# Two tiles of the gated merge move into the long convolution, and its table copies go

## The chip, the cores and the metric

One core of a Trainium2 chip runs the whole program in one launch. The metric is the device time of one execution in microseconds. The engines are TensorE (PE: matmuls and transposes), VectorE (DVE), ScalarE (ACT), GpSimd (POOL) and SyncE (SP), which only issues DMAs here. Each runs its own list of instructions in order, and they meet through semaphores.

## The reference

The program is a first block (layer norms, gated attention, a chunked recurrence, a feed-forward part) and a second one, for 512 tokens of width 1024 in float32. What matters here is the second block's mixer:

```python
y_na = neighbourhood_attention(...)            # 512 x 512
for n in range(2):                             # y_hy, 512 x 512
    z = gates[n] * long_conv_bidir(z, filt[:, 0, n], filt[:, 1, n], bias[n])
m = sigmoid(g_na) * (y_na @ w_na_o) + sigmoid(g_hy) * (y_hy @ w_hy_o)
x = x + g1 * (m @ w_out)
```

`y_na` is known before the convolution starts. `y_hy` is the result of its second pass (n = 1). The long convolution is done as products with tables of cosines and sines: forward into 512 frequencies, a product with the filter's spectrum, and back.

## The kernel before

**Arithmetic.** Every float32 product is split: each operand x becomes a high part (ScalarE rounds it to `fp32r`, a copy) and a low part (VectorE subtracts the high part from x), and TensorE forms high·high, high·low and low·high. `mm3` (L570 to L573) issues these three matmuls, one line each. `tile` (L600) is one 128 x 512 output tile: it waits for the weight's low part, takes one of TensorE's eight PSUM banks in rotation (waiting until its last content has been read), and issues 3 matmuls for each block of 128 of the contraction.

**Weights.** 1 MB pieces number 0 to 119 (`J_...`) go through three buffers `raw`. SyncE's `weights(upto)` issues the loads in order, each after the piece three before it has its low part. ScalarE's `high(upto)` and VectorE's `low_parts(upto)` split them in the same order, `low_parts` in 128 x 2048 subtractions. Most pieces alternate between two pairs `whi`/`wlo`; some (`OWN`) have a place of their own, given by `ahead`. A shared place is free when TensorE has passed `used` of the piece two before it.

**The long convolution** (`for n in range(2)`). The pieces J_DFT2 and J_DFT2 + 1 (77 and 78) hold the forward and the backward table. In pass n TensorE issues 16 forward products in four groups of frequencies f (`forward`), then 4 backward tiles `hi` (`back`): f = 0 for all four, f = 1 for all four, then f = 2 and 3 tile by tile. Between them, for each f, VectorE multiplies four times with the spectrum (signal `hp`), GpSimd forms two sums (`hsum`), ScalarE takes the high parts and VectorE the low parts `yy`. After pass 0 VectorE multiplies the `hi` tiles with a gate and filters (`hz`, source `x1` beside the banks), GpSimd sums, and ScalarE and VectorE split the sums into `zh` and `zl` (named `xrr` in the profile), the four inputs of pass 1; TensorE's first group of pass 1 goes through these inputs one after the other as they become ready. After pass 1 the tiles are combined (`kk`), gated and split to `zh`, `zl` again.

For pass 0 the tables lie in the shared places. After its part of pass 0 ScalarE copies all four halves (two high, two low) into `tabs` (signal `tab`), and pass 1 reads them there, so that the shared places are free for the merge's first weights. The copies stand on ScalarE between the high parts of pass 0's last frequencies and those of `zh`.

**The merge.** Its weights are J_MERGE (79, first half of the columns of w_na_o), 80 (first half of w_hy_o), 81 and 82 (second halves). For each half, `src` 0 takes `nh`, `nl` (the split y_na, named `Xr`) and `src` 1 takes `zh`, `zl`; each gives 4 tiles of 12 matmuls, and k numbers 8 output tiles. For each k the gates come from DRAM (`gd`, loaded by GpSimd's queue into `tq`), ScalarE takes the sigmoid, VectorE multiplies it with the bank (L2559), GpSimd adds the two sources, and ScalarE and VectorE split the sum into `tabs` again. ScalarE's `high` of piece 82 stands behind the high part of merged tile 3. Then the product with w_out begins (`J_OUT`), with `tabs` as moving operand.

**Loads.** SyncE issues 16 loads `kk` for the eight (n, f) with the three merge weights behind those of the seventh. GpSimd loads the row `bcg` behind the sums of the convolution.

Of the kernel before, what the change touches and what calls it, by code (L numbers as in the profile page):

```python
# [207 lines left out]
J_FAST = J_UP2 + 2  # L208
OWN = (*J_AHEAD, *range(J_TAP, J_TAP + 4), *range(J_FAST, J_FAST + N_FAST))
SHARED = [j for j in range(J_DOWN2 + 11) if j not in OWN]  # L210

# [82 lines left out]
def build(nc, ins, out):  # L294
    with ExitStack() as ctx:
# [15 lines left out]
        def flat(x):  # L311
            return x[:, :, :].rearrange("p a b -> p (a b)")
# [100 lines left out]
        with ExitStack() as c0:  # L413
# [77 lines left out]
        ahead = {J_WO + 3: (flat(qa_r), flat(ka_r)), J_UP + 2: (flat(qa_r), flat(ka_r)), J_K2: (flat(qn_r), flat(qt_r)),  # L491
                 J_UP2: (flat(cl), flat(act2_r[:, 0:4, :]))}

# [65 lines left out]
        def tensor_program(eng):  # L559
# [488 lines left out]


            for n in range(2):  # L1050
                if n == 0:
                    weights(J_DFT2)
                else:
                    pe.wait_ge(sig["tab"], 4)
                (fh, fl), (gh, gl_) = [parts_of(J_DFT2 + c) for c in range(2)] if n == 0 else tabs

# [46 lines left out]
                if n == 0:  # L1103
                    weights(J_DFT2 + 1)
                for k in range(4):
                    take(("hi", n, k), "hz", 24 + 3 * k + 2 if n else 16 + 4 * (k // 2) + 3 + k % 2)
# [6 lines left out]
                if n == 0:  # L1113
                    used(J_DFT2)
                    used(J_DFT2 + 1)


            for cgp in range(2):
                for src, (yh, yl, part) in enumerate(((nh, nl, "nh"), (zh, zl, "z1"))):
                    j = J_MERGE + 2 * cgp + src  # L1120
                    pe.wait_ge(sig["sp_lo"], split_no(part, 3))
                    for m in range(4):
                        tile(j, ("mg", src, 4 * cgp + m), "mg_m", 8 * cgp + 4 * src + m + 1, yh, yl, 0, m, nk=4, width=512)
                    used(j)
# [83 lines left out]
        def scalar_program(eng):  # L1208
# [22 lines left out]
            def high(upto):  # L1231

                while conv[0] <= min(upto, len(conv_at) - 1):
# [3 lines left out]
                    if j in (J_WO + 3, J_UP + 2):  # L1237
                        ac.wait_ge(sig["pe"], at["w", J_WO + 3 if j > J_WO + 3 else J_WO])
                    elif j == J_TAP:
                        ac.wait_ge(sig["h_ke"], 2)  # L1240
                        ac.wait_ge(sig["h_qe"], 2)
                    elif j == J_K2:
                        ac.wait_ge(sig["sp_lo"], split_no("down0", 7))
                    elif j == J_UP2:
                        ac.wait_ge(sig["pe"], at["w", J_MERGE + 3])
                    elif j in (J_DOWN2, J_DOWN2 + 1):
                        ac.wait_ge(sig["pe"], at["fast", N_FAST - 1 if j > J_DOWN2 else N_FAST - 2, last_of(N_FAST - 1 if j > J_DOWN2 else N_FAST - 2)])
                    elif j >= 2 and j != J_TAP + 1:
                        ac.wait_ge(sig["pe"], at["w", used_by(j)])
                    if j == J_DFT2 + 2:  # L1250
                        ac.wait_ge(sig["tab"], 4)
                    act(parts_of(j)[0], raw[i % 3][:, :], ACT.Copy, "whi")
# [414 lines left out]
            def mirrored_part(k):  # L1667
# [4 lines left out]
                act(bt[k % 2], b[:, 256:512], ACT.Copy, "zu")  # L1672

            def last_high(k):
                ac.wait_ge(sig["hz"], 24 + 3 * k + 3)
                act(zh[:, k, :], tq[k][:, :], ACT.Copy, "sp_hi")

            for n in range(2):
                if n:
                    tile(("hi", 0, 3))  # L1680
                for f in range(4):
                    sums_high(n, f)
                if n == 0:
                    for b in range(2):
                        ac.wait_ge(sig[f"tb{b}"], 16 * TB_ALL)
                    for c in range(2):
                        for i, x in enumerate(parts_of(J_DFT2 + c)):
                            act(tabs[c][i][:, :], x.bitcast(F32), ACT.Copy, "tab")
                for k in range(4):
# [6 lines left out]
                    else:  # L1696
                        mirrored_part(k)
                        if k:
                            last_high(k - 1)
                if n == 0:  # L1700
                    high(J_MERGE + 1)
                else:
                    last_high(3)
# [119 lines left out]
        def vector_program(eng):  # L1823
# [656 lines left out]
            for n in range(2):  # L2480
# [20 lines left out]
                sums_low(n, 3)  # L2501
                if n:
                    low_parts(J_MERGE)

# [46 lines left out]
            for cgp in range(2):  # L2551
                for src in range(2):
                    low_parts(J_MERGE + 2 * cgp + src + 1)
                    for m in range(4):
                        k = 4 * cgp + m
                        b = tile(("mg", src, k))
                        q = 4 + k % 3 if src else m
# [157 lines left out]
        def gpsimd_program(eng):  # L2715
# [222 lines left out]
            po.wait_ge(sig["gated"], 32)  # L2938
            po.wait_ge(sig["pe"], at["yt", 3])
            po.e.dma_start(bcg[:, :], rows_of(gated, 0)).then_inc(sig["rows"], 16)  # L2940
            def gate_first(k):
# [12 lines left out]
            for k in range(8):  # L2954
                po.wait_ge(sig["mg_m"], 8 * (k // 4) + 4 + k % 4 + 1)
                add(tq[k % 4][:, :], tq[4 + k % 3][:, :], tq[k % 4][:, :], ALU.add, "mg_a")
                if k < 5:
                    gate_second(k + 3)
                if k in (1, 2, 3):
                    gate_first(k + 3)  # L2960
# [51 lines left out]
        def sync_program(eng):  # L3012
# [72 lines left out]
            for k in range(8):  # L3085
                if k >= 3:
                    sp.wait_ge(sig["hp"], 4 * (k - 2))
                for i in range(2):
                    sp.e.dma_start(kk_[k % 3][:, i, :], kd[k // 4, 4 * i + k % 4]).then_inc(sig[f"kk{k % 3}"], 16)
                if k == 6:  # L3090
                    weights(conv_at[J_MERGE + 1] + 1)
            for k in range(4):
# [160 lines left out]
```

## Time and profile before

| | us |
|---|---|
| Median of 3 runs (1613.34 to 1614.63) | 1613.46 |
| The profiled execution | 1612.63 |
| its span in the trace | 1610.8 |
| TensorE busy | 1557.2 |
| granted clock of TensorE, mean | 0.993 |

The span runs from the first to the last instruction of the trace; all times of the rows are microseconds from its start. The profiled execution took 1.8 us more than its span. A matmul's length in the timeline includes its way through the array, so that consecutive ones overlap: what one costs in a row of many is the distance between their starts. The stretch that the diff touches lies between 1086 and 1199 us: attention ends at about 1092, pass 0 of the convolution lasts until 1120, pass 1 until 1155, and the merge until 1199.

### The profile page before, as it was taken

The numbers are of one execution on the slowest core, as the hardware profiler recorded it, in microseconds if no ns is written. First come the engines' busy times: TensorE is split into PE (matmuls) and PEld (weight loads), VectorE is DVE, ScalarE is ACT, GpSimd is POOL, SyncE is SP. The second block draws the span as 40 slices with busy tenths as digits, with TensorE's granted clock in tenths as the row PEclk, the third lists the DMA queues.
The fourth block names the chain that finished last, engine by engine and source line by source line (L and its number), as shares of the span: only waits on it lengthen the run. The fifth ranks groups of instructions, "written<-read, shape, count | busy, mean of one in ns | idle before, by whom it ended". The sixth has DMA issues, their size and how long they took to land. (4 is left out here: it accounts for less than half of the span.)

```text
span 1610.8 us, 21154 instructions
## 1 busy us (share of the span) xinstructions
PE 1557.2 (97%) x8536; PEld 1316.3 (82%) x8536; DVE 1006.4 (62%) x1453; ACT 698.7 (43%) x1022; POOL 429.0 (27%) x371
## 2 busy tenths in 40 slices
PE   6999998999999999999999999998899999999997
PEld 5768886788888887888988778886788999999886
DVE  7676456878887576325675643437864688885334
ACT  5644346736433333323623344444445544443322
POOL 0024325523421010000150022214332655550002
PEclk9999999999999999999999999999999999999999
DMA  7342112451444254321446432305452122224221
GB/s 301 105 144 92 66 72 79 158 212 75 157 167 149 108 205 157 105 105 66 142 158 260 133 99 90 115 34 177 147 192 106 53 106 105 106 105 157 82 76 53
DMA packets 46684, 202.05 MB, mean 125 GB/s; under 512 B 14480, under 2 KB 14736, under 8 KB 27962
## 3 DMA queue, kind: packets, MB, share of 16 engines
q1 hardware_dynamic: 37346, 172.04, 29.6%
q0 software_dynamic: 8704, 28.30, 5.0%
q8 instruction: 68, 1.11, 0.3%
q10 hardware_dynamic: 536, 0.35, 0.1%
q14 instruction: 30, 0.25, 0.0%
HBM read 179.67 MB, written 21.00 MB: 125 GB/s over the span
## 5 line engine op out<-in xcount | busy, mean ns | idle before, releaser
L571 PE MATMUL ps<-xh,whi 128*128 128x512 f32 (+1 forms) x1136 | 403.0, 355 | 11.3 <-DVE xl L1887 8.5
L572 PE MATMUL ps<-xl,whi 128*128 128x512 f32 (+1 forms) x1136 | 398.2, 350 | 0.0
L573 PE MATMUL ps<-xh,wlo 128*128 128x512 f32 (+1 forms) x1136 | 397.6, 350 | 0.0
L1843 DVE TENSOR_TENSOR wlo<-raw,whi 128x2048 fp32r<-128x2048 f32 x91 | 222.3, 2443 | 143.9 <-ACT whi L1213 143.8
L1213 ACT ACTIVATE whi<-raw 128x512 fp32r<-128x512 f32 (+1 forms) x193 | 236.8, 1231 | 160.1 <-PE ps L573 90.0
L571 PEld LDWEIGHTS ps<-xh,whi 128*128 128x128 f32 x1136 | 216.1, 190 | 51.9 <-issue 22.2
L573 PEld LDWEIGHTS ps<-xh,wlo 128*128 128x128 f32 x1136 | 215.1, 189 | 30.0
L572 PEld LDWEIGHTS ps<-xl,whi 128*128 128x128 f32 x1136 | 215.3, 190 | 27.6
L2719 POOL TENSOR_TENSOR act<-xr 128x512 f32<-128x512 f32 x22 | 39.9, 1817 | 198.2 <-DVE xr L2285 197.6
L2285 DVE SCALAR_TENSOR_TENSOR xr<-ps,pc,xr 128x511 f32<-128x511 f32 x88 | 65.2, 747 | 40.8 <-ACT xr L1213 39.3
L2615 DVE TENSOR_TENSOR wlo<-raw,whi 128x512 fp32r<-128x512 f32 x98 | 79.0, 838 | 0.0
L1213 ACT ACTIVATE xr<-ps,pc 128x512 f32<-128x512 f32 x44 | 34.0, 772 | 94.1 <-PE ps L573 94.0
L573 PE MATMUL ps<-whi,al 128*128 128x512 f32 x176 | 69.8, 397 | 0.0
L571 PE MATMUL ps<-whi,ah 128*128 128x512 f32 x176 | 69.8, 397 | 0.0
L572 PE MATMUL ps<-wlo,ah 128*128 128x512 f32 x176 | 69.8, 397 | 0.0
L1213 ACT ACTIVATE xr<-xr 128x512 f32<-128x512 f32 (+1 forms) x31 | 23.5, 757 | 83.7 <-DVE xr L2285 59.0
L2152 DVE TENSOR_SCALAR cl<-ps,st 128x64 f32<-128x64 f32 x32 | 9.0, 281 | 73.8 <-PE ps L816 73.8
L571 PE MATMUL ps<-whi,xh 128*128 128x512 f32 x128 | 52.0, 407 | 1.1 <-DVE vr L1958 1.1
L2719 POOL TENSOR_TENSOR tq<-tq 128x512 f32<-128x512 f32 x28 | 39.8, 1439 | 49.1 <-DVE tq L2559 22.0
L2634 DVE TENSOR_TENSOR xr<-ps,xr 128x256 f32<-128x256 f32 (+1 forms) x63 | 33.8, 536 | 30.4 <-PE ps L573 29.9
L572 PE MATMUL ps<-wlo,xh 128*128 128x512 f32 x128 | 50.7, 396 | 0.0
L573 PE MATMUL ps<-whi,xl 128*128 128x512 f32 x128 | 50.7, 396 | 0.0
(468 smaller groups left out, 3500.7 us busy)
## 6 DMA issues: line engine op xcount, KB each, us to landing
raw<-in_w_in SPq DMA_DIRECT2D x35, 1024.0 KB, 5.2
raw<-in_ffn_w SPq DMA_DIRECT2D x33, 1024.0 KB, 4.8
raw<-in_ada SPq DMA_DIRECT2D x24, 1024.0 KB, 4.8
raw<-in_w_up SPq DMA_DIRECT2D x22, 1024.0 KB, 5.0
raw<-in_w_down SPq DMA_DIRECT2D x11, 1024.0 KB, 4.7
xd<-X POOLq DMA_DIRECT2D x8, 512.0 KB, 6.6
td<-vr POOLq DMA_DIRECT2D x16, 256.0 KB, 3.5
raw<-td SPq DMA_DIRECT2D x4, 1024.0 KB, 4.8
```

The lines of the kernel that those rows point to most:

```text
L571: pe.e.matmul(o, lh, rh, start=start, stop=False)
L572: pe.e.matmul(o, lh, rl, start=False, stop=False)
L573: return pe.e.matmul(o, ll, rh, start=False, stop=stop)
L1213: m = ac.e.activation(dst, src, func, **more)
L1843: up(ve.e.tensor_tensor(lo, raw[conv_at[j] % 3][:, :], hi.bitcast(F32), ALU.subtract), "wlo")
L2152: up(ve.e.tensor_scalar(dst, b[:, hcol:hcol + 64], st[:, i % 32, 3:4], None, ALU.mult), "at_o")
L2285: up(ve.e.scalar_tensor_tensor(out=y[:, o], in0=b[:, i], scalar=pcol(name + "_w", n * w + c), in1=y[:, o], op0=ALU.mult, op1=ALU.add), "cv ...
L2615: up(ve.e.tensor_tensor(lo, product_source(n, p), hi.bitcast(F32), ALU.subtract), "wlo")
L2634: up(ve.e.tensor_tensor(dst, b, s, ALU.add), "f_a")
L2719: po.e.tensor_tensor(dst, a, b, op).then_inc(sig[signal], 1)
```

## The change

Two of the merge's sixteen tiles (source 0, tiles 0 and 1) are computed inside the convolution: tile 0 on TensorE behind pass 0, tile 1 in pass 1 between the forward and the backward part. ScalarE copies their banks into `x1`, from where VectorE's later product with the sigmoid reads them. The pieces 79 and 80 get places of their own: 79 where the table copies were, 80 in `bc` and `cl`. The four copies of the tables go, and both passes read the shared places. On ScalarE the high part of piece 79 stands where the copies were; VectorE takes its low part at the end of pass 0's frequencies, and the low part of 80 at the end of pass 1's. Loads of 79, 80 and 81 are issued behind the third, fifth and seventh pair of `kk`. The load of `bcg` moves to GpSimd's fifth step of the merge.

The places of the pieces:

```diff
-OWN = (*J_AHEAD, *range(J_TAP, J_TAP + 4), *range(J_FAST, J_FAST + N_FAST))
+OWN = (*J_AHEAD, J_MERGE, J_MERGE + 1, *range(J_TAP, J_TAP + 4), *range(J_FAST, J_FAST + N_FAST))
...
-                 J_UP2: (flat(cl), flat(act2_r[:, 0:4, :]))}
+                 J_UP2: (flat(cl), flat(act2_r[:, 0:4, :])),
+                 J_MERGE: (tabs[1][0][:, :], tabs[1][1][:, :]), J_MERGE + 1: (bc_r[:, :], flat(cl))}
```

TensorE's program:

```diff
+            def first_merge(m):
+                tile(J_MERGE, ("mg", 0, m), "tab", m + 1, nh, nl, 0, m, nk=4, width=512)
...
-                else:
-                    pe.wait_ge(sig["tab"], 4)
-                (fh, fl), (gh, gl_) = [parts_of(J_DFT2 + c) for c in range(2)] if n == 0 else tabs
+                (fh, fl), (gh, gl_) = [parts_of(J_DFT2 + c) for c in range(2)]
...
                 if n == 0:
                     weights(J_DFT2 + 1)
+                else:
+                    first_merge(1)
                 for k in range(4):
                     take(("hi", n, k), "hz", 24 + 3 * k + 2 if n else 16 + 4 * (k // 2) + 3 + k % 2)
...
                 if n == 0:
-                    used(J_DFT2)
-                    used(J_DFT2 + 1)
+                    first_merge(0)
+            used(J_DFT2)
+            used(J_DFT2 + 1)
...
-                    for m in range(4):
+                    for m in range(0 if src or cgp else 2, 4):
```

ScalarE's:

```diff
+                    elif j == J_MERGE:
+                        for b in range(4):
+                            ac.wait_ge(sig[f"tb{b}"], 16 * TB_ALL)
+                        ac.wait_ge(sig["pe"], at["yt", 3])
...
+            def first_merged(m):
+                b = tile(("mg", 0, m))
+                ac.wait_ge(sig["hz"], 24)
+                act(x1[:, m, :], b[:, :], ACT.Copy, "tab")
...
                     sums_high(n, f)
+                    if n and f == 1:
+                        first_merged(1)
                 if n == 0:
-                    for b in range(2):
-                        ac.wait_ge(sig[f"tb{b}"], 16 * TB_ALL)
-                    for c in range(2):
-                        for i, x in enumerate(parts_of(J_DFT2 + c)):
-                            act(tabs[c][i][:, :], x.bitcast(F32), ACT.Copy, "tab")
+                    high(J_MERGE)
...
                 if n == 0:
+                    first_merged(0)
                     high(J_MERGE + 1)
```

VectorE's:

```diff
-                if n:
-                    low_parts(J_MERGE)
+                low_parts(J_MERGE + n)
...
-                        b = tile(("mg", src, k))
+                        if src or k >= 2:
+                            b = tile(("mg", src, k))
+                        else:
+                            ve.wait_ge(sig["tab"], m + 1)
+                            b = x1[:, m, :]
```

GpSimd's:

```diff
-            po.wait_ge(sig["pe"], at["yt", 3])
-            po.e.dma_start(bcg[:, :], rows_of(gated, 0)).then_inc(sig["rows"], 16)
...
+                if k == 4:
+                    po.wait_ge(sig["pe"], at["w", J_MERGE + 1])
+                    po.e.dma_start(bcg[:, :], rows_of(gated, 0)).then_inc(sig["rows"], 16)
```

SyncE's:

```diff
-                if k == 6:
-                    weights(conv_at[J_MERGE + 1] + 1)
+                if k in (2, 4, 6):
+                    weights(conv_at[J_MERGE + k // 2 - 1])
```

## Rows read from the trace of the kernel before

**Rows 1.** The page: span; busy time of TensorE, its share, instructions.
```profile
span 1610.8 us, 21154 instructions
...
PE 1557.2 (97%) x8536; PEld 1316.3 (82%) x8536; DVE 1006.4 (62%) x1453; ACT 698.7 (43%) x1022; POOL 429.0 (27%) x371
```

**Rows 2.** Windows: length, busy time (instructions) per engine, PEclk, DMA share, GB/s.
```profile
1090.00:1155.00 65.00, 52.87 (x273) 43.03 (x272) 56.17 (x77) 29.88 (x38) 29.84 (x22) 0.97 0.44 147
1155.00:1250.00 95.00, 95.00 (x436) 78.02 (x435) 55.09 (x67) 47.47 (x65) 28.77 (x31) 1.00 0.44 155
1148.50:1152.00 3.50, 3.50 (x19) 3.50 (x18) 3.14 (x4) 0.38 (x1) 0.00 (x0) 0.52 0.99 310
```

**Rows 3.** Timeline, TensorE: start, length, instruction; in brackets idle and releaser.
```profile
1120.20 0.40 PE L573 MATMUL ps<-yy,wlo 128*128 128x512 f32 x1
...
1122.89 0.47 PE L571 MATMUL ps<-xrr,tab 128*128 128x512 f32 x1 [2.29 <-DVE xrr L1857]
...
1128.82 0.50 PE L571 MATMUL ps<-xrr,tab 128*128 128x512 f32 x1 [0.88 <-DVE xrr L1857]
...
1135.52 0.39 PE L573 MATMUL ps<-xrr,tab 128*128 128x512 f32 x1
...
1137.43 0.36 PE L571 MATMUL ps<-tab,yy 128*128 128x256 f32 x1 [1.52 <-DVE yy L1857]
...
1142.13 0.39 PE L571 MATMUL ps<-tab,yy 128*128 128x256 f32 x1 [1.61 <-DVE yy L1857]
...
1154.75 0.39 PE L571 MATMUL ps<-Xr,whi 128*128 128x512 f32 x1
...
1165.67 0.40 PE L571 MATMUL ps<-xrr,whi 128*128 128x512 f32 x1
...
1187.81 0.40 PE L571 MATMUL ps<-xrr,whi 128*128 128x512 f32 x1
...
1199.01 0.39 PE L571 MATMUL ps<-whi,tab 128*128 128x512 f32 x1
```

**Rows 4.** Timeline, VectorE, convolution and merge.
```profile
1117.89 2.48 DVE L2519 TENSOR_TENSOR tq<-ps,ch 128x512 f32<-128x512 f32 x4 [2.51 <-PE ps L573]
1120.71 1.29 DVE L2519 TENSOR_TENSOR tq<-ps,ch 128x512 f32<-128x512 f32 x2 [0.33 <-PE ps L573]
1122.05 2.38 DVE L1857 TENSOR_TENSOR xrr<-tq,xrr 128x512 fp32r<-128x512 f32 x2
...
1137.21 2.47 DVE L2498 TENSOR_TENSOR tq<-ps,kk 128x512 f32<-128x512 f32 x4
...
1158.17 1.48 DVE L1857 TENSOR_TENSOR xrr<-tq,xrr 128x512 fp32r<-128x512 f32 x2
...
1182.47 2.29 DVE L1843 TENSOR_TENSOR wlo<-raw,whi 128x2048 fp32r<-128x2048 f32 x1 [1.11 <-ACT whi L1213]
```

**Rows 5.** Timeline, ScalarE, convolution and merge.
```profile
1114.20 1.90 ACT L1213 ACTIVATE tab<-whi 128x2048 fp32r<-128x2048 f32 x1
...
1127.94 3.70 ACT L1213 ACTIVATE whi<-raw 128x2048 fp32r<-128x2048 f32 x2
...
1139.89 0.63 ACT L1213 ACTIVATE yy<-tq 128x512 fp32r<-128x512 f32 x1 [2.49 <-POOL tq L2719]
...
1163.56 1.30 ACT L1213 ACTIVATE tq<-tq 128x512 f32<-128x512 f32 x2 [2.17 <-DMA tq<-gd]
1165.93 1.92 ACT L1213 ACTIVATE whi<-raw 128x2048 fp32r<-128x2048 f32 x1 [1.07 <-PE ps L573]
```

**Rows 6.** Timeline, GpSimd, end of the first convolution.
```profile
1119.26 2.53 POOL L2719 TENSOR_TENSOR tq<-tq 128x512 f32<-128x512 f32 x2 [5.63 <-DVE tq L2519]
1122.08 1.80 POOL L2719 TENSOR_TENSOR tq<-tq 128x512 f32<-128x512 f32 x1 [0.28 <-DVE tq L2519]
```

**Rows 7.** Timeline, SyncE's DMA queue.
```profile
1086.73 25.88 SPq L3089 DMA_DIRECT2D kk<-kd  x14
```

**Rows 8.** By tile, the weights w_na_o: issue to landing.
```profile
DMA to landing us min/median/max: 8.5/10.5/12.4
```

More of the change, by code:

```diff
@@ L1247, in high @@
                         ac.wait_ge(sig["pe"], at["fast", N_FAST - 1 if j > J_DOWN2 else N_FAST - 2, last_of(N_FAST - 1 if j > J_DOWN2 else N_FAST - 2)])
-                    elif j >= 2 and j != J_TAP + 1:
+                    elif j == J_MERGE:
+                        for b in range(4):
+                            ac.wait_ge(sig[f"tb{b}"], 16 * TB_ALL)
+                        ac.wait_ge(sig["pe"], at["yt", 3])
+                    elif j >= 2 and j not in (J_TAP + 1, J_MERGE + 1):
                         ac.wait_ge(sig["pe"], at["w", used_by(j)])
-                    if j == J_DFT2 + 2:
-                        ac.wait_ge(sig["tab"], 4)
                     act(parts_of(j)[0], raw[i % 3][:, :], ACT.Copy, "whi")
```

## The prediction

> **What bounds the kernel now.** I read the page first: TensorE is busy in 97% of the span [rows 1], so only a change that takes work or a wait off TensorE's own list can move the end. Then the windows: from 1090 to 1155 us it is busy in 52.87 of 65, and from 1155 to 1250 in 95 of 95 [rows 2]. So the convolution is bound by the chain of TensorE, VectorE, GpSimd and ScalarE, while in the merge TensorE works without a pause. The timeline of TensorE shows the pauses that the diff aims at. Its last backward matmul of pass 0 starts at 1120.20, and pass 1 begins at 1122.89 after 2.29 us idle; its first group has another pause of 0.88 ahead of 1128.82. The last forward matmul of pass 1 starts at 1135.52, the backward part at 1137.43 after 1.52, and its second frequency at 1142.13 after 1.61 [rows 3]. All are waits for low parts from VectorE. Last I read the other engines around these places [rows 4 to 6].
>
> **The tiles leave the merge.** Four tiles of source 0 take 1154.75 to 1165.67, 10.92 us, so one takes 2.73, and the two that go give 5.46 [rows 3]. That is the whole gain if the places where they are put cost nothing.
>
> **Tile 0, behind pass 0.** TensorE is free for it about 0.23 (estimate, one matmul's distance: 2.73 / 12) behind 1120.20, at 1120.43, and done at 1123.2. Pass 1 began at 1122.89, so its first matmuls are 0.3 late. The pause of 0.88 before the fourth input's products at 1128.82 takes this up [rows 3]: cost 0. Without that cover it would be 0.3. Its weights must be split by then. ScalarE's high part stands where the first table copy started, 1114.20, and takes 1.90 [rows 5]; the low part takes 2.29 [rows 4] and so ends at about 1118.5, 1.9 before TensorE needs it. The load is issued behind three pairs of `kk` that start at 1086.73 [rows 7]; even with the longest landing of this tensor, 12.4 [rows 8], it has landed long before 1114.
>
> **Tile 1, in pass 1.** It starts at 1135.75 and ends at 1138.5, 1.05 behind the old start of the backward part at 1137.43. The rotation of banks also moves on by two: the fourth `hi` bank is now one whose content is read by the third product of the block that VectorE starts at 1137.21 and ends at 2.47 later [rows 4], so about 1139.1, and `take` stands ahead of all four tiles. The backward part then starts near 1139.2, 1.8 late, where the pause before 1142.13 covers 1.61 [rows 3]. That leaves 0.2, which the like pause of the third frequency (VectorE's same loop) takes up, so cost 0; bounds 0 and 0.2, and the whole 1.8 if those pauses were not there. ScalarE's copy of the bank stands before the high part that starts at 1139.89 after 2.49 idle [rows 5]; TensorE ends the tile at 1138.5, the copy needs 0.6, and it fits with half a microsecond to spare. In pass 0 the other copy replaces ScalarE work: only one of the two 128 x 2048 copies of 3.70 at 1127.94 stays [rows 5].
>
> **The cost: VectorE at the end of pass 0.** The four table copies were ScalarE's, and the first high part behind them was not what VectorE waited for: VectorE came to it from its own products at 1122.05 [rows 4]. Taking the copies away therefore gives nothing on the chain. The new 2.29 low part does cost. It runs from about 1116.2 to 1118.5, and the block of four products that started at 1117.89 (after 2.51 idle) starts 0.6 late; that ends at 1121.0 where the next block started at 1120.71, so the chain is 0.25 to 0.3 late [rows 4]. Behind it stand the low parts of pass 1's inputs. There two subtractions took 2.38 where two others took 1.48 [rows 4], and GpSimd's sum beside them took 1.80 where two took 2.53, 1.27 each [rows 6]; they met. A shifted meeting can cost another 0.9 or save that. So the delay d of all of pass 1 lies between -0.6 and 1.15; I take 0.6, near the middle of the unlucky half, since the sums are now closer to the subtractions.
>
> The row shows that the two collide. The Trainium skill (SBUF — State Buffer, "Who interferes with whom") says why: a VectorE operation with both inputs in SBUF and a GpSimd operation that reads SBUF exclude each other, each for its whole length. By that rule the long low part would block GpSimd for 2.29 if a sum fell into it, and the two products that now read `x1` in place of a bank become such operations too; by the rows GpSimd is idle for 5.63 before 1119.26 [rows 6], so the sum by the rule stays as it is, with d at 0.6.
>
> **The merge.** TensorE enters it at 1154.75 + 0.6, does two tiles, then source 1 from 1160.8, for which the last low part of pass 1 is there at 1158.17 + 1.48 + 0.6 = 1160.3 [rows 3, 4]. Then tiles 4 to 7 until it needs piece 82 at 1187.81 - 5.46 + 0.6 = 1182.95 [rows 3]. Its low part started at 1182.47 and took 2.29, ending 1184.8, 3.0 before use [rows 4]; unmoved, it would now cost 1.8. But it moves: ScalarE's high part of piece 81 waited for TensorE at 1165.93, although its sigmoids at 1163.56 were done by 1164.86 [rows 5]. The new condition is met at 1155, and the sigmoids' own wait for a load is shorter by some tenths because the 1 MB loads come earlier. So the chain from there on is 1.1 to 1.8 ahead, and piece 82 is ready between 1183.0 and 1183.7. I take a wait of 0.1; bounds 0 and 1.8. What follows (product with w_out, norms, feed-forward) waits for TensorE and moves as one. `bcg` is loaded later, but used only behind the product with w_out. Queue entries on GpSimd: one less in the convolution, one more in the merge, where it waits for VectorE anyway.
>
> Sum at an unchanged clock: 5.46 - 0.6 - 0.1 = 4.8.
>
> **The clock.** From 1148.5 to 1152.0 the granted clock was 0.52, the lower of its two levels (1.2 GHz) [rows 2]. It fell after a stretch with three pauses of 1.5 us and more. Its 19 matmuls of 256 columns took 3.50. At full clock they would take 2.3 (estimate: 24 of them run from 1137.43 to 1142.13 - 1.61 = 1140.5, 0.12 each) [rows 2, 3], so 1.2 was lost. With tile 1 the two pauses ahead of this shrink from 3.1 to about 0.7, so I expect the drop to go. The gain is not whole: piece 82's chain hangs on ScalarE's and VectorE's work, and TensorE runs into it earlier, so I give back half. 4.8 + 0.6 = 5.4.
>
> The Trainium skill (TensorE: Matmul & The Clock Gate, "What's actually happening") has the clock follow how busy TensorE has recently been. By it the drop goes, as here; without it the sum stays at 4.8.
>
> **From the profile to the median.** The sum is made against the profiled execution of 1612.63, whose span is 1610.8. The median of the runs is 1613.46, 0.8 more, and the difference is taken from that: 1613.46 - 5.4 = 1608.1.
>
> **Rivals.**
> A (the forecast): tiles hidden, the clock drop gone. 1608.1, chance 0.40; its own range 1607 to 1609.3.
> B: tiles hidden, the drop stays, since other pauses of pass 1 stay. 4.8 less, 1608.7, chance 0.30.
> C: the merge turns from TensorE's to the gates' chain (loads of `gd`, sigmoid, product, sum, split, then piece 82). For it: the sigmoids at 1163.56 waited for a load [rows 5], and that wait is set by the z parts of pass 1, which move later, not earlier. Against it: 1.1 us of room in front of 1165.93. If piece 82 is ready no sooner than before, TensorE starts on it at 1184.8 in place of 1187.81: 3.0 gained, 1610.4. Chance 0.17.
> D, slower: piece 79's split is late. TensorE and VectorE take their lists in order, and both have work of pass 1 behind it; on VectorE these are the four products of 1117.89, so it costs from there. A landing at L gives a low part that ends at L + 1.90 + 2.29 + 0.1, and pass 1 is late by what this is beyond 1118.2 (1117.89 and the 0.33 idle before 1120.71) [rows 4, 5]. The 5.46 are eaten up when L is 1119.4. A load issued where the fourteenth `kk` ends, 1086.73 + 25.88 = 1112.61, would be there at 1123.1 with 10.5 us landing [rows 7, 8]: 9.2 late, 3.7 slower than before, 1617.2. Against it: the issue stands behind the third pair, not the seventh. Chance 0.05.
> E: more than A, when the meeting of VectorE and GpSimd falls well and the whole 1.2 of the clock is kept: 6.6, 1606.9. Chance 0.08.
>
> **The numbers.** The range goes from 1606.6 to 1611.0: E's end below and C's above. A difference under 0.2%, 3.2 us, can't be told from none. Faster by more: A, B, E and nearly none of C, 0.77. Within: C and the upper end of B, 0.18. Slower: 0.05.
>
> **What would show it.** The pauses before 1122.89 and 1137.43 hold twelve matmuls each. The first products of VectorE behind pass 0 start some 0.6 later; the first matmul of the fourth input of pass 1 at 1129.1 to 1129.9. The merge begins at about 1155 and w_out's product at 1193.5 to 1194.5. PEclk is 1.00 in pass 1's backward part (A) or not (B). A pause ahead of piece 82 over 1 us is C. A pause ahead of tile 0 is D. I am wrong if w_out's product starts at the forecast time but the end does not follow, or if pass 1 grows by more than 2 us.

## The result, and the profile after

The changed kernel takes 1608.47 us (median of 7 runs, 1606.93 to 1611.45), the kernel before 1614.3 beside it (7 runs, 1612.93 to 1616.39). The ratio is 0.9972, interval 0.9961 to 0.9983: faster, by 2.7 to 6.3 us. A second comparison, later, gave 1610.48 (11 runs) against 1614.17 (33 runs), 0.9974 [0.9965, 0.9983]. The forecast was 1608.1, 5.4 less than the 1613.46 that the kernel before had then.

The profiled execution took 1610.57, and its page shows TensorE as busy as before [rows 1]:

```profile
span 1608.8 us, 21150 instructions
...
PE 1558.5 (97%) x8536; PEld 1316.6 (82%) x8536; DVE 1002.3 (62%) x1453; ACT 692.4 (43%) x1020; POOL 428.8 (27%) x371
```

The windows of the profile after (columns as in [rows 2]): the convolution's window has 57.67 us of TensorE where it had 52.87, and the clock is low behind 1148.5 here too. The last two lie outside the change.

```profile
1090.00:1155.00 65.00, 57.67 (x294) 47.05 (x294) 57.06 (x76) 24.07 (x35) 29.32 (x21) 0.97 0.43 146
1155.00:1250.00 95.00, 95.00 (x457) 78.79 (x456) 53.95 (x72) 50.70 (x72) 29.28 (x32) 1.00 0.48 171
1148.50:1152.00 3.50, 3.02 (x18) 2.82 (x19) 3.50 (x4) 0.69 (x2) 0.00 (x0) 0.80 0.73 212
515.00:535.00 20.00, 20.00 (x93) 18.02 (x93) 7.04 (x9) 2.57 (x2) 2.54 (x2) 0.66 0.43 159
1275.00:1285.00 10.00, 8.79 (x61) 8.82 (x62) 9.28 (x11) 4.90 (x10) 6.21 (x4) 0.83 0.31 107
```

TensorE's timeline after, which answers to [rows 3] (first and last matmul of each tile moved, and the matmul behind it):

```profile
1122.18 0.39 PE L572 MATMUL ps<-Xr,tab 128*128 128x512 f32 x1
...
1124.76 0.39 PE L574 MATMUL ps<-Xr,tab 128*128 128x512 f32 x1
1124.99 0.40 PE L572 MATMUL ps<-xrr,whi 128*128 128x512 f32 x1
...
1130.62 0.49 PE L572 MATMUL ps<-xrr,whi 128*128 128x512 f32 x1 [0.85 <-DVE xrr L1868]
...
1137.72 0.39 PE L572 MATMUL ps<-Xr,tab 128*128 128x512 f32 x1
...
1140.30 0.39 PE L574 MATMUL ps<-Xr,tab 128*128 128x512 f32 x1
1141.15 0.35 PE L572 MATMUL ps<-whi,yy 128*128 128x256 f32 x1 [0.47 <-DVE tq L2509]
...
1148.75 0.38 PE L572 MATMUL ps<-whi,yy 128*128 128x256 f32 x1 [1.66 <-DVE yy L1868]
...
1156.56 0.40 PE L572 MATMUL ps<-Xr,tab 128*128 128x512 f32 x1
...
1162.17 0.39 PE L572 MATMUL ps<-xrr,bcr 128*128 128x512 f32 x1
...
1184.27 0.39 PE L572 MATMUL ps<-xrr,whi 128*128 128x512 f32 x1
...
1195.46 0.39 PE L572 MATMUL ps<-whi,tab 128*128 128x512 f32 x1
```

No pause stands ahead of 1124.99, where 2.29 us stood; ahead of the backward part 0.47 is left of 1.52, and the 1.61 behind it is gone. From 1156.56 on there is no pause. VectorE after, which answers to [rows 4]:

```profile
1098.91 4.87 DVE L2509 TENSOR_TENSOR tq<-ps,kk 128x512 f32<-128x512 f32 x8 [0.57 <-issue]
...
1117.87 2.29 DVE L1854 TENSOR_TENSOR tab<-raw,tab 128x2048 fp32r<-128x2048 f32 x1 [0.75 <-ACT tab L1218]
1120.08 3.67 DVE L2529 TENSOR_TENSOR tq<-ps,ch 128x512 f32<-128x512 f32 x6
1123.67 0.86 DVE L1868 TENSOR_TENSOR xrr<-tq,xrr 128x512 fp32r<-128x512 f32 x1
1124.69 1.55 DVE L1868 TENSOR_TENSOR xrr<-tq,xrr 128x512 fp32r<-128x512 f32 x1 [0.15 <-ACT xrr L1218]
...
1159.77 1.48 DVE L1868 TENSOR_TENSOR xrr<-tq,xrr 128x512 fp32r<-128x512 f32 x2
...
1181.72 2.29 DVE L1854 TENSOR_TENSOR wlo<-raw,whi 128x2048 fp32r<-128x2048 f32 x1 [1.11 <-ACT whi L1218]
```

And GpSimd's three sums beside the two subtractions [rows 6]:

```profile
1121.44 4.24 POOL L2733 TENSOR_TENSOR tq<-tq 128x512 f32<-128x512 f32 x3 [6.07 <-DVE tq L2529]
```

**A yardstick finer than the runs.** Runs of one kernel differ by 3 to 11 us, single terms are under 3. So I measure a *stretch* in each trace: from the first of the last sixteen transposes of the attention (`ps<-ident,cl`; 1092.02 before, 1093.41 after) to w_out's first matmul (1199.01 and 1195.46). It is 106.99 before and 102.05 after: 4.94 shorter. The span is only 2.0 shorter, since the start lies 1.39 later and the way from w_out to the end takes 413.34 in place of 411.79. Both have a clock row. From 515 to 535 us the clock is 0.66, where the kernel before has 0.74:

```profile
515.00:535.00 20.00, 20.00 (x100) 17.90 (x99) 7.45 (x10) 3.35 (x3) 2.53 (x2) 0.74 0.41 159
```

TensorE's matmul number 2401 starts at 484.27 (484.46 before), number 2801 at 574.20 (572.80 before), so 1.59 is lost between them. From 1275 to 1285 the clock is 0.83, and 1.00 before. Offsets below ("+37.21") count from the stretch's start.

### The profile page after: what moved, and what is told of

Its sections match the earlier page's. It is cut to its first block and busy times, and to the rows that moved or that the text cites. A ratio compares the mean times of both kernels' runs of the same rounds, so it can differ in the third digit from the quotient of the medians.

```text
span 1608.8 us, 21150 instructions
## 1 busy us (share of the span) xinstructions
PE 1558.5 (97%) x8536; PEld 1316.6 (82%) x8536; DVE 1002.3 (62%) x1453; ACT 692.4 (43%) x1020; POOL 428.8 (27%) x371
## 5 line engine op out<-in xcount | busy, mean ns | idle before, releaser
L1854 DVE TENSOR_TENSOR wlo<-raw,whi 128x2048 fp32r<-128x2048 f32 x89 | 217.5, 2444 | 142.5 <-ACT whi L1218 142.4
L1218 ACT ACTIVATE whi<-raw 128x512 fp32r<-128x512 f32 (+1 forms) x191 | 233.0, 1223 | 156.8 <-PE ps L574 86.8
```

What stands on the lines that cost most here:

```text
L1218: m = ac.e.activation(dst, src, func, **more)
L1854: up(ve.e.tensor_tensor(lo, raw[conv_at[j] % 3][:, :], hi.bitcast(F32), ALU.subtract), "wlo")
```

## The experiments

Each is the changed kernel with the edit shown (ScalarE's copies of the banks and VectorE's reading of them follow it); "pause 5" is TensorE's 1.6 us ahead of the third frequency of pass 1's backward part (1148.75 above).

**Tile 0 alone.**
```diff
-                else:
-                    first_merge(1)
...
-                    for m in range(0 if src or cgp else 2, 4):
+                    for m in range(0 if src or cgp else 1, 4):
```


> Only tile 0 stands in the convolution (behind pass 0); tile 1 is back in the merge; places, loads and splits are those of the change. The stretch from the last transposes of attention to the first matmul with w_out was 106.99 us before and 102.05 with the change. Theory (each tile is hidden wholly, 2.73 us each): 104.8 us, and a time 2.7 us above the change's. Rival (the gain comes from the places and loads, not the tiles): 102 to 102.5. Rival (tile 0 is the one that costs, since pass 1 is a chain): 106.5, no gain left over from it.

Measured: stretch 104.46, 2.53 shorter than before, with the clock low (0.51 from 1148.5 to 1152), near the theory's 104.8; from w_out on 413.34. The runs: 1613.57, ratio 0.9997 [0.9987, 1.0006].

**Tile 1 alone.**
```diff
-                if n == 0:
-                    first_merge(0)
...
-                    for m in range(0 if src or cgp else 2, 4):
+                    for m in (range(4) if src or cgp else (0, 2, 3)):
```


> Only tile 1 stands in the convolution (pass 1), tile 0 is in the merge. Theory: the same 104.8 us for the stretch as with tile 0 alone; the pause ahead of pass 1 is back (about 2.3 us) and the wait for the bank ahead of the backward part stays at 0.4 to 0.5. Rival (tile 1 costs through the rotation of banks): 105.5 to 106.

Measured: stretch 103.19, below theory and rival, since the clock is full at 1150; the pause ahead of pass 1 is back with 2.30, the one ahead of the backward part is 0.47. The clock is low here behind the 2.30, in pass 1's first group, where consecutive matmuls start 0.43 apart and not 0.23. The fourth input comes at +37.08 even so, 0.28 later than before, of which 0.25 come from pass 0: the pause ahead of it took the low clock's loss up. Runs: 1611.87, 0.9996 [0.9985, 1.0007].

**No tile moved, the table copies gone, piece 79 split in pass 0.**
```diff
-                    first_merge(0)
...
-                    first_merge(1)
...
-                    for m in range(0 if src or cgp else 2, 4):
+                    for m in range(4):
```


> Neither tile stands in the convolution; the table copies are gone and pieces 79 and 80 have their places, loads and splits as in the change. This shows what the rest of the change costs or gives by itself. Theory: the stretch takes 107.4 us, 0.4 to 0.5 more than before: 0.36 for the store of the gates that VectorE's first products wait for (the early 1 MB load shares the DMA engines with it), about 0.05 for the low part in pass 0. Rival (the copies' removal gives something): under 106.7. Rival of the prediction (VectorE's low part costs 0.6 or more): over 107.9.

Measured: stretch 107.48, 0.49 longer than before; pauses 2.30, 0.86, 1.34, 1.61, 1.66 in pass 1. Runs: 1614.78, 1.0002 [0.9989, 1.0014]. Pass 0 came 0.19 late here (below), so what the change does beside the tiles costs another 0.3, of which 0.03 shows at the fourth input; the rest lies in source 0's first four tiles (11.25 against 10.92), and why is open. It gains nothing. Against this kernel, each with its lateness of pass 0 taken off, tile 0 gives 2.83 and the two give 5.58, all three at the low clock at 1150: about their own 2.73 each. Both are hidden whole, and they add up. The runs' medians couldn't have told this: they place both single tiles level with before. Part of that is the low clock at 1275 to 1285, which both have and which takes some 1.5 back behind the stretch; the rest is open.

**Pause 5 filled** with seven matmuls whose result the next tile overwrites.
```diff
+                if n:
+                    h, _ = weights(J_MERGE)
+                    pe.wait_ge(sig["tab"], 2)
+                    for q in range(7):
+                        pe.e.matmul(bank["mg", 0, 1][:, :], h[:, P * q:P * q + P], nh[:, 0, :], start=True, stop=True)
                 for k in range(4):
                     for f in (2, 3):
                         back(f, k)
```


> The change with seven matmuls of 512 columns more whose results are overwritten, ahead of the third frequency's backward part of pass 1, where TensorE waits 1.66 us. Theory of the prediction (the clock drop at about 1150 follows from TensorE's pauses in pass 1): the drop to 0.5 is gone from 1148 to 1156, the backward part ends 1.2 us earlier, and the stretch is 101.0 to 101.6. Rival (the drop does not hang on these pauses): the drop is there and the stretch 102.0 to 102.2, no pause to fill being left over 0.1.

Measured: the drop is gone, as the theory has it, the stretch is 100.89 (1.16 less than the change's, of which 0.34 is that pass 0 isn't late here), and there is a pause that the change doesn't have, for the low part of piece 82:

```profile
1184.86 0.51 PE L572 MATMUL ps<-xrr,whi 128*128 128x512 f32 x1 [0.34 <-DVE wlo L1859]
```

Runs: 1610.33, 0.9983 [0.9973, 0.9992].

**The low part of piece 79 computed twice**, the second time as the change does.
```diff
+                if n == 0:
+                    ve.wait_ge(sig["whi"], conv_no(J_MERGE))
+                    ve.e.tensor_tensor(tabs[0][1][:, :], raw[conv_at[J_MERGE] % 3][:, :], parts_of(J_MERGE)[0].bitcast(F32), ALU.subtract)
                 low_parts(J_MERGE + n)
```


> The change with one more 128 x 2048 subtraction (2.29 us) on VectorE just ahead of piece 79's low part in pass 0, its result unused. The change's own low part moved VectorE's next products by 0.44 us but pass 1's fourth input by only 0.05. Theory (the first 0.3 to 0.4 vanish in the meeting of VectorE's and GpSimd's SBUF operations, everything beyond goes through): the products start 2.2 later and the stretch from attention's last transposes to the first matmul with w_out grows from 102.05 to 104.0 to 104.3, with a new pause ahead of tile 0. Rival (there is more room in the chain): under 103.

Measured, on VectorE and at the two pauses of TensorE in pass 1:

```profile
1118.99 2.29 DVE L2515 TENSOR_TENSOR tab<-raw,tab 128x2048 fp32r<-128x2048 f32 x1 [0.75 <-ACT tab L1218]
1121.20 2.28 DVE L1854 TENSOR_TENSOR tab<-raw,tab 128x2048 fp32r<-128x2048 f32 x1
1123.40 3.07 DVE L2532 TENSOR_TENSOR tq<-ps,ch 128x512 f32<-128x512 f32 x5
```
```profile
1127.98 0.47 PE L572 MATMUL ps<-xrr,whi 128*128 128x512 f32 x1 [1.37 <-DVE xrr L1868]
...
1133.91 0.50 PE L572 MATMUL ps<-xrr,whi 128*128 128x512 f32 x1 [0.86 <-DVE xrr L1868]
```

The fourth input comes at +39.04 where tile 0 alone has +36.88: 2.16 of the extra 2.2 go through. VectorE has no slack behind pass 0. The new pause is ahead of pass 1 (1.37), not ahead of tile 0 as expected. The stretch is 103.51, between theory and rival, with full clock at 1150 and at 1275; runs 1611.05, 0.9983 [0.9972, 0.9995].

**The load of piece 79 issued behind all pairs of `kk` but the last.**
```diff
-                if k in (2, 4, 6):
-                    weights(conv_at[J_MERGE + k // 2 - 1])
+                if k == 6:
+                    weights(conv_at[J_MERGE + 1] + 1)
```


> The change with the loads of pieces 79, 80 and 81 all behind the seventh pair of kk loads, where they stood before. Rival D of the prediction, made to happen: the load of 79 lands some 8 to 12 us after about 1114, ScalarE's and VectorE's split and with them the products behind pass 0 start 8 to 9 us late; the stretch is 109.5 to 111.5 against 106.99 before and 102.05 with the change, and the kernel is 1 to 4 us slower than before. Rival (the load is faster here because nothing is beside it, landing in 5 us): 105 to 106.5, still a gain.

Measured: the load was issued at 1111.68; ScalarE waited for it, and TensorE stood ahead of tile 0, not of pass 1:

```profile
1118.38 1.92 ACT L1218 ACTIVATE tab<-raw 128x2048 fp32r<-128x2048 f32 x1 [5.07 <-DMA raw<-in_w_nao]
```
```profile
1122.68 0.79 PE L572 MATMUL ps<-Xr,tab 128*128 128x512 f32 x1 [3.05 <-DVE tab L1854]
```

It landed 6.7 us after its issue. The fourth input came at +42.02, 4.8 later than in the change and 5.2 later than before. The stretch is 106.87, between theory and rival, and the runs 1613.32, 0.9997 [0.9988, 1.0006]: the gain is gone, and not more. Rival D's mechanism is real; it had 9.2 late, of which 3.8 are the landing of 10.5 in place of 6.7.

**A third tile in pause 5.**
```diff
+                if n:
+                    tile(J_MERGE, ("mg", 0, 2), "mg_m", 3, nh, nl, 0, 2, nk=4, width=512)
                 for k in range(4):
                     for f in (2, 3):
                         back(f, k)
...
-                    for m in range(0 if src or cgp else 2, 4):
+                    for m in range(0 if src or cgp else 3, 4):
```


> The change with a third tile (tile 2 of source 0) on TensorE ahead of the third frequency's backward part of pass 1, where it waits 1.66 us; its bank is read later as before. Theory (what is left is bound by the chain behind pass 1, whose last low part ends 0.9 ahead of its use, and by piece 82, ready 0.25 ahead): TensorE comes to source 1 early and waits 1 to 2 us there; the stretch is 101.6 to 102.2, the third tile giving nearly nothing. Rival (each tile put into a pause gives 2.73 less its overshoot of 0.8): 100.1 to 100.3.

Measured: full clock at 1150, and two pauses in the merge, the first somewhat above the theory's 1 to 2 us:

```profile
1156.67 0.50 PE L572 MATMUL ps<-xrr,bcr 128*128 128x512 f32 x1 [2.20 <-DVE xrr L1870]
...
1179.71 0.51 PE L572 MATMUL ps<-xrr,whi 128*128 128x512 f32 x1 [0.66 <-DVE wlo L1856]
```

Stretch 101.24, 0.35 longer than with pause 5 filled for nothing; runs 1610.69, 0.9979 [0.997, 0.9988]. Of the tile's 2.73, 2.20 is waited for ahead of source 1, whose last low part doesn't come sooner (+66.90 here, +66.84 with pause 5 filled).

**Third tile in two halves, in pause 5 and behind the backward part; the loads of 79 and 80 both behind the fourth pair of `kk`, piece 82 split one tile earlier.**
```diff
+            def third_merge(k0):
...
+                for k in range(k0, k0 + 2):
+                    a = 512 * k + 2 * P
+                    o = mm3(b[:, :], h[:, a:a + P], l[:, a:a + P], nh[:, k, :], nl[:, k, :], k == 0, k == 3)
...
+                if n:
+                    third_merge(0)
                 for k in range(4):
                     for f in (2, 3):
                         back(f, k)
+                if n:
+                    third_merge(2)
...
-                    for m in range(0 if src or cgp else 2, 4):
+                    for m in range(0 if src or cgp else 3, 4):
...
-                if k in (2, 4, 6):
-                    weights(conv_at[J_MERGE + k // 2 - 1])
+                if k in (3, 4, 6):
+                    weights(conv_at[J_MERGE + k // 2 - (k > 3)])
...
+                    if m == 2 and cgp == 0:
+                        high(J_MERGE + 3)
...
+                        if k == 3 and src:
+                            low_parts(J_MERGE + 3)
```


> The change with three edits: the load of piece 79 one pair of kk later (theory: gives back the 0.36 us that VectorE waits for the store of the gates), piece 82 split before merged tile 0 (ScalarE) and before merged tile 3's low part (VectorE), and the first six of tile 2's twelve matmuls in the 1.66 us pause of pass 1, the other six behind pass 1. Theory: the stretch is 100.7 to 101.0 if the clock drop at about 1150 is there, 100.0 to 100.3 if not, against 102.05 and 100.89. Rival (nothing left to gain, source 1's input sets the pace): 101.7 or 100.5.

Measured: the stretch is the shortest, 100.28, as foreseen for a full clock at 1150, with no pause ahead of piece 82. But from w_out on it takes 420.62. TensorE, ScalarE and the windows there:

```profile
1211.37 0.79 PE L572 MATMUL ps<-whi,tab 128*128 128x512 f32 x1 [4.99 <-DVE wlo L1871]
```
```profile
1188.90 0.63 ACT L1233 ACTIVATE tq<-tq 128x512 f32<-128x512 f32 x1 [4.35 <-DMA tq<-gd]
...
1202.31 0.63 ACT L1233 ACTIVATE tq<-tq 128x512 f32<-128x512 f32 x1 [5.99 <-DMA tq<-gd]
```
```profile
1200.00:1205.00 5.00, 5.00 (x23) 4.03 (x22) 1.51 (x3) 1.67 (x3) 0.14 (x1) 1.00 1.00 374
1210.00:1216.00 6.00, 4.63 (x11) 3.67 (x12) 3.52 (x2) 0.79 (x1) 0.00 (x0) 0.50 0.58 216
```

The early split does two things. It frees a buffer, so w_out's 1 MB load goes out at 1182.22 (1184.04 in the change). And it holds VectorE, so GpSimd waits 1.64 us for VectorE and issues its 256 KB load of gates at 1183.09 (1180.90 in the change, ahead of the big load). Issued behind the big load, the gates take 5.8 us to land, where they took 3.5 in the change:

```profile
1183.09 0.55 POOL L2975 DMA_DIRECT2D tq<-gd  x1 [1.64 <-DVE tab L1885]
```

The next gates load is therefore issued at 1195.95, beside 2 MB of `X<-xd`, and takes 6.3. Behind it hangs the next split of w_out, 4.99 us late, and behind the pause the clock is 0.50. Runs: 1612.93, 0.9994 [0.9982, 1.0007].

**The change again.** The same kernel, unedited.

> The changed kernel itself, beside other runs of the one before, for the size of the gain and a second profile. Theory: 0.9970 to 0.9975 of the time before (4 to 5 us less); the stretch from attention's last transposes to the first matmul with w_out is 101.7 to 102.1 where the clock drop at about 1150 is there and 100.9 to 101.0 where it is not. Rival (the gain of the first seven runs was luck of the clock): under 2.5 us less.

Measured: neither of the two. Stretch 102.34 at full clock from 1148 to 1156, with a wait for piece 82:

```profile
1148.00:1156.00 8.00, 7.24 (x54) 6.81 (x55) 7.79 (x13) 3.18 (x7) 0.03 (x1) 1.00 0.86 286
1275.00:1285.00 10.00, 9.26 (x65) 9.29 (x65) 9.26 (x10) 4.79 (x9) 6.51 (x4) 0.83 0.31 107
```
```profile
1183.70 0.50 PE L572 MATMUL ps<-xrr,whi 128*128 128x512 f32 x1 [0.94 <-DVE wlo L1854]
```
```profile
1098.68 4.88 DVE L2509 TENSOR_TENSOR tq<-ps,kk 128x512 f32<-128x512 f32 x8 [1.09 <-issue]
```

Of this kernel there are thus two traces, one with the low clock and one without. From the backward part to source 1 the first takes 21.02 (1141.15 to 1162.17), the second 19.37 (1141.03 to 1160.40): with the low clock it takes 1.65 more (0.08 of it pause 5). From source 1 to w_out the first takes 33.29, the second 34.60: 1.31 comes back, 0.94 of it as this pause, the rest without a pause of its own. The last row shows why the stretch is no shorter even so: VectorE's first products started 0.52 later still than in the first trace.

**Before again.** The kernel before, unedited.

> The kernel before, for a second profile. Theory: the stretch is again 106.9 to 107.1 with the clock drop at about 1150 or 105.7 without; from the first matmul with w_out to the end it took 411.8 in its first profile and 413.3 in that of the change and of five of its variants, always with a clock drop at 1275 to 1285. Theory: that drop has nothing to do with the change, and falls on this kernel too in some executions (413.3). Rival: the kernel before always shows 411.8, and the change brings the drop.

Measured: stretch 107.02 with the low clock at 1150, 411.81 from w_out on, both within 0.03 of the first trace. So the low clock at 1275 to 1285 is again absent, as the rival has it; two traces don't settle whether this kernel ever has it. Runs: 1612.52 (8 runs), 0.9996 [0.9985, 1.0007] against the others of the same kernel: the method finds no difference where there is none.

**The third tile in halves and the moved loads, piece 82 as in the change.** The edit of the two halves without its last two hunks.

> The last version without the early split of piece 82: the load of 79 one pair later and six of tile 2's matmuls in the pause of pass 1. With the early split there was a pause of 4.99 us in the product with w_out. Theory (the early split freed its buffer early, the next 1 MB load then met the loads of the gates, one of these landed 5 to 6 us late, and so on to the split of J_OUT + 1): the pause is gone, 411.8 or 413.3 us from the first matmul with w_out to the end; the stretch before it is 100.8 to 101.1, with 1.0 to 1.3 us of waiting ahead of source 1 and some tenths ahead of piece 82. Rival (the six matmuls in the pause bring it about): the pause of some 5 us is there.

```profile
1160.31 0.50 PE L572 MATMUL ps<-xrr,bcr 128*128 128x512 f32 x1 [1.17 <-DVE xrr L1883]
...
1183.20 0.50 PE L572 MATMUL ps<-xrr,whi 128*128 128x512 f32 x1 [0.53 <-DVE wlo L1869]
```

Measured: pause 5 is 0.30, the clock full at 1150, the stretch 101.06, and from w_out on 413.3: the pause there is gone, so it came with the early split and not with the six matmuls. Runs: 1609.71, 0.9969 [0.9959, 0.9979], the best ratio here, though not apart from the change's 0.9974.

**The moved loads and the early split of piece 82 alone.** The last three hunks of the same edit.

> The change with the load of 79 one pair later and the early split of piece 82, without the third tile's part. Theory: the late landings of the gates and the pause of 4 to 5 us in the product with w_out are there, 417 to 421 us from its first matmul to the end, and the kernel is 2 to 5 us slower than the change. Rival: the pause needs TensorE's earlier arrival too and is absent, 411.8 or 413.3.

```profile
1207.87 0.50 PE L572 MATMUL ps<-whi,tab 128*128 128x512 f32 x1 [2.03 <-DVE wlo L1856]
```

Measured: stretch 101.75 with the low clock at 1150, but 414.16 from w_out on, with this pause; runs 1612.2, 0.9991 [0.9978, 1.0004]. The collision comes with the early split alone, here at a smaller size than expected (2.03 against 4.99; 414.16 against 417 to 421). Both moves are there again: w_out's load at 1180.52, and the gates behind it at 1181.39 after the same 1.64 of waiting for VectorE, landing 5.95 later. Whether one of the two would do alone was not run.

## Why the prediction was right, step by step

- **The tiles leave the merge (5.46).** The merge with its two tiles less takes 38.90 (1156.56 to 1195.46) where it took 44.26 [rows 3]: 5.36. Shown; the missing 0.1 has no pause behind it.
- **Tile 0 at no cost.** Pass 1 began 0.37 late, beside the 0.34 of pass 0 (forecast 0.3), and the pause ahead of the fourth input went from 0.88 to 0.85, since both TensorE and VectorE moved. Shown by the kernel with this tile alone.
- **Tile 1 at no cost.** The backward part begins 1.92 late against the fourth input (forecast 1.8), for `tq<-ps` of the bank's third product, as named. From the fourth input to the merge the traces take 25.93 and 25.94: cost 0.01.
- **VectorE's low part, d = 0.6: mis-sized.** With the 0.34 of the next point taken off, the products started at +26.33 against +25.87 before, 0.46 late, but the fourth input at +36.87 against +36.80, only 0.07. The two subtractions took 0.86 and 1.55, nearly the 2.38 of before, yet met the sums (4.24 for three) otherwise; that it was the meeting that won the rest back is argued. The doubled low part shows that a longer delay of this chain goes through whole.
- **A term that I did not have: 0.34 in pass 0.** I asked only whether the early load of piece 79 lands in time, not what it stands beside. VectorE's first product of pass 0 comes behind a wait for the stores of the gates (`tb0` to `tb3`), and the last of them, `gd<-tm`, is issued by GpSimd in the same microsecond as this load. From its issue to its landing, before and in the change:

```profile
DMA to landing us min/median/max: 5.0/5.0/5.0
```
```profile
DMA to landing us min/median/max: 7.4/7.4/7.4
```

In the change it landed at 1098.63, and the product started 0.28 behind it, at 1098.91, after the idle 0.57 that the row puts down to "issue"; the whole pass came 0.34 late. In the second trace the store took 7.9, the wait was 1.09 and the pass 0.87 late. The store took 6.3 to 7.9 in the eight traces with the load behind the third pair. In the four where it took over 7 the product followed the landing by 0.27 or 0.28 and the pass was late by 0.2 to 0.9 (the change twice, tile 1 alone, no tile); in the other four 6.3 was still in time. In the six with the load elsewhere, the two of the kernel before among them, it took 4.6 to 5.5 and no pass is late. So this term is a price of the early load, paid in some executions and not in others; with the load one pair later it was paid in none of three traces.
- **Piece 82, wait 0.1.** Its low part ended at 1184.01 and TensorE needed it at 1184.27: 0.26 to spare, within the bounds of 0 to 1.8. At full clock it was late (0.94 and, in other kernels, 0.34, 0.81, 0.66, 0.53). It doesn't come sooner when TensorE does: in the two traces of the change it ends at +90.60 and, less the 0.53 of pass 0, at +90.46. This is rival C's mechanism, one step behind the present bound.
- **The clock: the step that failed.** "I expect the drop to go" did not hold in the profiled run (0.80 in the window of [rows 2]; the low stretch now lies from 1150.5 to 1154.1). It went in the second trace of the same kernel. Low clock near 1150 stands in 7 of the 10 traces with pause 5, and in none of the 4 in which the pause was filled. That points to pause 5, which the change leaves at 1.66, but 4 traces don't prove it, and the two shrunken pauses were not enough. What it is worth was right in kind: 1.65 lost, and 1.31 of it given back by piece 82's chain, where I gave back half of 1.2. So A and B differ by 0.3 us, not by 0.6, and the forecast could not hang on it.
- **From the stretch to the end.** The terms add up: 5.36 - 0.01 - 0.07 - 0.34 = 4.94, against 4.8 that I had without the clock. In the profiled run 1.39 and 1.55 of it were lost outside the stretch, near 520 us and at 1275 to 1285, where the clock is lower than before. Both come and go. The 0.66 near 520 stands in both traces of the change and in six of its ten variants, in neither of before. The low clock at 1275 stands in both traces of the change, in eight of the variants, the kernel without a tile among them, and in neither of before; it is absent from the doubled low part. Whether the change brings either is open. The medians' differences, 5.8 and 3.7, lie on both sides of 4.9.

The signs named in advance fit as well, counted from the stretch's start: the fourth input came 0.41 later than before (forecast 0.3 to 1.1), the merge began 0.42 later (about 0.3), and w_out's product 4.94 earlier (4.5 to 5.5). Sum and end met because the too large d and the missing 0.34 cancelled, and the clock's net worth was small. That the first median fell within 0.4 us of the forecast is luck: the second, of the same kernel, lies 2.4 above it, still inside the range.

## What to carry over

When an engine takes its list in order, work of a later stage may be put into its waits; an overshoot costs nothing as long as the next wait downstream is longer, so look at that wait and not only at the one being filled. Then ask which chain now ends last: here it was 0.26 us behind, and a third tile bought next to nothing. A load or a split that is moved earlier is in time, but it also meets what it did not meet before: look at which small store or load will stand beside the big one, and at who waits for the engine that now does the split first. And where runs differ by more than the term in question, measure a stretch of the trace with fixed ends, once more for each kernel.

## What the runs showed of the hardware

- The same kernel ran through the same pauses once with a low clock behind them and once at full clock. The Trainium skill (TensorE: Matmul & The Clock Gate, "What's actually happening") says of a kernel's start that the number of slow matmuls varies from run to run of one kernel; these two traces show the like in its middle, with 1.65 us between them.
- The early split of piece 82 took 3.38 us on VectorE where the same operation takes 2.29 elsewhere. VectorE and GpSimd in the kernel with the two halves:

```profile
1178.81 3.38 DVE L1871 TENSOR_TENSOR wlo<-raw,whi 128x2048 fp32r<-128x2048 f32 x1
```
```profile
1178.55 1.49 POOL L2752 TENSOR_TENSOR tq<-tq 128x512 f32<-128x512 f32 x1
```

The sum covers the first 1.23 of it, and it is 1.09 too long. The Trainium skill (SBUF — State Buffer, "Who interferes with whom") has two such operations exclude each other. By that the 1.23 in common would be lost; 1.09 was.
- A 256 KB load issued by GpSimd took 5.8 and 6.3 us to land beside loads of 1 and 2 MB issued by SyncE, where the change's like loads of that place took 2.9 to 3.5. A store by GpSimd took 4.6 to 5.5 without, and 6.3 to 7.9 with, a 1 MB load issued within half a microsecond of it. A load of 1 MB took 6.7 us in one place and up to 12.4 in another [rows 8]: a landing time from one place is a poor price for another.
